# A fused fp32 transformer kernel on one core: router in plain fp32 with the tokens as stationary side, routing reordered, and the layer ends rearranged

## What is computed

```python
def grouped_moe(x, w_router, b_router, w_gate, w_up, w_down):        # first block, twice
    scores = softmax(x @ w_router + b_router)
    grp = scores.reshape(-1, 4, 4)
    g_sel = argmax(sum(top_k(grp, 2)[0], -1))                          # the best group
    top_w, top_i = top_k(grp[g_sel], 2); top_w = top_w / sum(top_w)
    for e in range(16):
        y = y + gate[:, e:e + 1] * ((silu(x @ w_gate[e]) * (x @ w_up[e])) @ w_down[e])

def hier_moe(h, w_rg, b_rg, w_re, b_re, w_gate, w_up, w_down):         # second block
    g_sel = argmax(softmax(h @ w_rg + b_rg)); e_val, e_idx = top_k((h @ w_re + b_re)[g_sel], 2)
# after it, in the second block:
    x = x + sigmoid(x @ w_ple_gate) * (p @ w_ple_proj)
```

## Time and profile before

| | us |
|---|---|
| median of 3 runs (lowest, highest) | 1481.27 (1480.82, 1482.70) |
| the profiled execution | 1480.01 |
| its span from the first to the last instruction | 1478.3 |
| PE, PEld, DVE, ACT, POOL busy | 1396.9, 1000.5, 607.5, 498.2, 53.8 |
| mean granted clock of TensorE | 0.982 |
| share of the chain that ended last: PE, DVE, ACT, issue | 88%, 5%, 4%, 2% |

### The profile page before, as it was taken

The page is one execution under the profiler, slowest core; times in us unless marked ns, Lnnn a source line. Parts: engine busy times, 40 slices in busy tenths (PEclk is TensorE's granted clock), DMA queues, the critical chain, the costliest instruction groups (busy, mean ns, idle before and its releaser), DMA issues.

```text
span 1478.3 us, 20927 instructions
## 1 busy us (share of the span) xinstructions
PE 1396.9 (94%) x8927; PEld 1000.5 (68%) x8927; DVE 607.5 (41%) x1001; ACT 498.2 (34%) x695; POOL 53.8 (4%) x95
## 2 busy tenths in 40 slices
PE   7999998999997999998999999799999989999977
PEld 5788976555554788986655554788787765555546
DVE  4677435111114585646111111657766561111124
ACT  5454434111113544443211111466565331111123
POOL 5000000000001000000000000000000000000000
PEclk9999999999999999999999999999999999999989
DMA  9556458999999455647899999453443769999970
GB/s 326 198 166 205 148 212 327 423 421 421 421 420 343 139 170 171 206 168 311 331 420 421 421 420 410 172 171 115 142 143 129 280 248 412 421 421 420 421 294 29
DMA packets 90807, 422.71 MB, mean 286 GB/s; under 512 B 7068, under 2 KB 7232, under 8 KB 53840
## 3 DMA queue, kind: packets, MB, share of 16 engines
q1 hardware_dynamic: 86528, 407.92, 70.8%
q0 software_dynamic: 4176, 13.30, 2.6%
HBM read 420.15 MB, written 1.05 MB: 285 GB/s over the span
## 4 chain that ended last, share of the span: by engine, by line
PE 88%; DVE 5%; ACT 4%; issue 2%; POOL 0%; DMA 0%; DVEq 0%; POOLq 0%; ACTq 0%
PE ps L1055 23%; PE ps L1091 12%; PE ps L753 5%; PE ps L754 5%; PE ps L758 5%; PE ps L972 4%; PE ps L1103 4%; PE ps L867 3%; PE ps L801 3%; PE ps L874 3%; PE ps L868 3%; PE ps L802 3%; PE ps L806 3%; PE ps L1080 1%; PE ps L914 1%
## 5 line engine op out<-in xcount | busy, mean ns | idle before, releaser
L1782 DVE TENSOR_TENSOR raw_low<-raw,w_high 128x1024 fp32r<-128x1024 f32 x198 | 237.4, 1223 | 171.2 <-ACT w_high L1440 170.5
L1440 ACT ACTIVATE w_high<-raw 128x1024 fp32r<-128x1024 f32 x198 | 206.6, 1058 | 258.6 <-PE ps L758 115.2
L2067 DVE TENSOR_TENSOR hid<-silu_g,ps 128x256 f32<-128x256 f32 x48 | 29.6, 616 | 259.8 <-PE ps L1055 259.8
L753 PE MATMUL ps<-w_high,act_high 128*128 128x512 f32 x272 | 110.6, 407 | 6.4 <-DVE raw_low L1782 3.6
L2075 DVE SCALAR_TENSOR_TENSOR out_low<-ps,stats,out_high 128x512 fp32r<-128x512 f32 x48 | 36.1, 751 | 182.3 <-ACT out_high L1546 182.3
L754 PE MATMUL ps<-raw_low,act_high 128*128 128x512 f32 x272 | 108.4, 399 | 0.0
L758 PE MATMUL ps<-w_high,act_low 128*128 128x512 f32 x272 | 103.3, 393 | 0.0
L1055 PE MATMUL ps<-raw,own_odd 128*64 128x256 f32 x800 | 91.6, 380 | 0.0
L1546 ACT ACTIVATE out_high<-ps,stats 128x512 fp32r<-128x512 f32 x48 | 33.0, 687 | 161.5 <-PE ps L1091 161.5
L867 PE MATMUL ps<-act_high,w_high 128*128 128x256 f32 x288 | 81.7, 287 | 5.4 <-issue 3.4
L1541 ACT ACTIVATE spread<-ps 128x288 fp32r<-128x288 f32 x48 | 19.7, 411 | 186.7 <-PE ps L1080 186.7
(11 more groups left out here) (411 smaller groups left out, 2570.8 us busy)
## 6 DMA issues: line engine op xcount, KB each, us to landing
raw<-in_w_up SPq DMA_DIRECT2D x46, 1024.0 KB, 11.3
raw<-in_w_in SPq DMA_DIRECT2D x44, 1024.0 KB, 9.2
raw<-in_w_gate SPq DMA_DIRECT2D x44, 1024.0 KB, 13.1
raw<-in_w_down SPq DMA_DIRECT2D x41, 1024.0 KB, 16.7
work<-in_w_down SPq DMA_DIRECT2D x23, 1024.0 KB, 19.7
work<-in_w_gate SPq DMA_DIRECT2D x21, 1024.0 KB, 7.9
w_lent<-in_w_gate SPq DMA_DIRECT2D x18, 1024.0 KB, 13.0
w_lent<-in_w_down SPq DMA_DIRECT2D x14, 1024.0 KB, 14.8
```

What stands on the lines that cost most here:

```text
L753: pe.matmul(bank[:, t, :], xh, wh, start=(k == 0), stop=False)
L1440: A(split_unit(n)[0], raw_unit(n), ACT.Copy).then_inc(high_ready, 1)
L1782: V.tensor_tensor(split_unit(n)[1], raw_unit(n), split_unit(n)[0].bitcast(F32), ALU.subtract).then_inc(low_ready, 1)
```

## The change

The diff, cut to its core:

```diff
-        plan_in(slots, L + turned_input + "0", L + turned_input + "1", L + "routerT", L + "router", L + "pos")
+        plan_in(slots, L + turned_input + "0", L + turned_input + "1", L + "router", L + "pos")
...
-    plan_job("2.x2T0", "2.x2T1")
-    plan_dense([a["w_ple_proj_2"][0].rearrange("(c p) n -> p c n", p=P)], "2.pp0", "2.pp1")
-    plan_dense([rows(a["w_ple_gate_2"][0], j) for j in range(4)], "2.pg0", "2.pg1")
+    plan_dense([a["w_ple_proj_2"][0].rearrange("(c p) n -> p c n", p=P)], "2.pp0", "2.pp1", slots=(H_SLOT, Y_SLOT))
+    plan_in(SUM_SLOTS, "2.x2T0", "2.x2T1")
+    plan_dense([rows(a["w_ple_gate_2"][0], j) for j in range(4)], "2.pg0", "2.pg1", slots=SUM_SLOTS)
...
-        NARROW = DEPTH * RANK + 2 * NE + SH + 4
+        NARROW = DEPTH * RANK + SH
+        router_w = sb("router_w", [P, KC, 2 * NE + 4])
...
+            def router(name, names, m, c0, width):
+
+                begin(name)
+                for t in range(TT):
+                    pe.wait_ge(S["front_turned"], TT * m + t + 1)
+                    pe.wait_ge(S["back_turned"], TT * m + t + 1)
+                    for c in range(KC):
+                        i = pe.matmul(slot_ps(name)[:, t * width:t * width + width], tokens_T[:, c, t * P:t * P + P], router_w[:, c, c0:c0 + width],
+                                      start=(c == 0), stop=(c == KC - 1))
+                        if c == 0:
+                            frees(i, names[t])
+                full(i, name)
...
                 for s in range(SLOTS):
                     pe.wait_ge(free[s], moe_at[m][1][s])
+                for _ in range(2):
+                    pe.matmul(ps[:, 1, 0:T], ident[:], tri[:, 0, :], start=True, stop=True)
...
-                    turn_tiles(x, (L + "xT0", L + "xT1"), S["normed"], TT * (3 * l - 1), idle=(8, 0))
-                dense_cols(L + "qk", head=(L + "xT0", L + "xT1"))
+                    turn_tiles(x[:, 0:1, :], (L + "xT0",), S["normed"], TT * (3 * l - 1))
+                second = (lambda: turn_tiles(x[:, 1:2, :], (L + "xT1",), S["normed"], TT * (3 * l - 1) + 1)) if l else None
+                dense_cols(L + "qk", head=(L + "xT0", L + "xT1"), between=second)
...
-            turn_tiles(h_tok, ("2.xT0", "2.xT1"), S["normed"], TT * 3 * DEPTH, idle=(14, 0))
+            turn_tiles(h_tok, ("2.xT0", "2.xT1"), S["normed"], TT * 3 * DEPTH)
...
-            turn_tiles(x, ("2.x2T0", "2.x2T1"), S["moe_added"])
             operand_ready("2.pT")
             dense_rows(("2.pp0", "2.pp1"), 1, (p_high, p_low))
+            turn_tiles(x, ("2.x2T0", "2.x2T1"), S["moe_added"])
...
                 for e in range(NE + 2):
                     if e >= 2:
                         output(e - 2)
+                    if e == NE:
+                        split(SPLIT - LATE)
...
-                    tiles_high(act_high, names[t:t + 1], t)
+                    wait_full(act, names[t])
+                    A(tokens_T[:, 0:KC // 2, t * P:t * P + P], slot_banks(names[t])[:, 0, :].rearrange("p (c s) -> p c s", s=P),
+                      ACT.Copy).then_inc(S["front_turned"], 1)
                     A(regrouped(x_tok[0][:, t, :]), runs(src[:, t, :]), ACT.Copy).then_inc(S["tok_high"], 1)
-                    A(y_acc[:, t, :], x[:, t, :], ACT.Copy, scale=scale).then_inc(S["residual_ready"], 1)
+                    if t == 0:
+                        residual_copied(0, scale)
...
-                narrow_copied(L + "router", NE, routT)
                 act.wait_ge(S["router_max"], l + 1)
                 A(probs, probs, ACT.Exp).then_inc(S["router_exp"], 1)
+                residual_copied(1, ALPHA)
...
                 V.tensor_tensor(probs, e_logits, r_max.to_broadcast([P, TT, NE]), ALU.subtract).then_inc(S["router_max"], 1)
+                ranks(groups(e_logits))
                 dve.wait_ge(S["router_exp"], l + 1)
-                ranks(groups(probs))
...
-                V.tensor_reduce(most, src[:, TT * NE:(TT + 1) * NE], AX, ALU.max)
-                frees(V.tensor_tensor(at_place, src[:, 0:TT * NE].rearrange("p (t n) -> p t n", t=TT), pick, ALU.mult), name)
+                link(V.tensor_tensor(at_place, src[:, 0:TT * NE].rearrange("p (t n) -> p t n", t=TT), pick, ALU.mult))
+                chosen(0, 0).then_inc(picks_made[m], 1)
+                frees(V.tensor_reduce(most, src[:, TT * NE:(TT + 1) * NE], AX, ALU.max), name)
+                chosen(0, 1)
                 wait_released(dve, name)
-                choose(0).then_inc(picks_made[m], 1)
...
                     if 0 < e <= NE:
                         hidden_copied(e - 1)
+                    if e == NE:
+                        split(HEAD)
...
                 route_one(l)
+                token_low(1, x, l)
                 place(l)
+                gates_one()
```

More of the change, by code:

```diff
@@ L741, in high_made, with dense_cols @@
                     pe.wait_ge(S["turned_high"], turn_no[name])
-            def dense_cols(name, src=MAIN, after_two=None, head=None):
+            def dense_cols(name, src=MAIN, after_two=None, head=None, between=None):
                 nonlocal n
@@ L762, in dense_cols @@
                     for t in range(TT):
+                        if t == 1 and between is not None:
+                            between()
                         high_made(head[t])
@@ L936, in narrow_turned @@
                     pe.matmul(dst, nl[:, c, :], act_high[:, c, 0:T], start=False, stop=False)
-                if head is not None:
-                    operand_ready(*head)
                 for c in range(KC):
@@ L1280, in _ @@
                 turn_tiles(x, (L + "x2T0", L + "x2T1"), S["normed"], TT * (3 * l + 1), idle=(2, 7))
-                narrow(L + "router", N_R, NE, (L + "x2T0", L + "x2T1"), routT)
+                router(L + "router", (L + "x2T0", L + "x2T1"), l, 0, NE)
                 sums_started(l)
@@ L1409, in _ @@
             turn_tiles(h_tok, ("2.x1T0", "2.x1T1"), S["normed"], TT * (3 * DEPTH + 2), idle=(2, 4))
-            narrow("2.router", N_RE, NE + 4, ("2.x1T0", "2.x1T1"), routT)
+            router("2.router", ("2.x1T0", "2.x1T1"), DEPTH, NE, NE + 4)
             sums_started(DEPTH)
@@ L1555, in experts_own @@
                         places_turned(e)
-                split(2)
                 if m == DEPTH:
@@ L1993, in choose, with chosen @@
             def choose(q):
-                for t, h in ((t, h) for t in range(TT) for h in range(2)):
+                for h in range(2):
+                    i = chosen(q, h)
+                return i
+            def chosen(q, h):
+                for t in range(TT):
                     i = V.tensor_tensor(picked[q % 2][:, t, :, h, :], slot_no[:].unsqueeze(1).to_broadcast([P, QUAD, OWN]),
@@ L2384, in _ @@
             route_two()
+            token_low(1, h_tok, DEPTH)
             place(DEPTH)
```

120 lines of the change are left out of this document (60 added, 60 removed).

## The result

| | before | after |
|---|---|---|
| median of 5 runs each, us (lowest, highest) | 1481.27 (1479.59, 1483.57) | 1493.53 (1486.78, 1495.41) |
| the profiled execution, and its span | 1480.01, 1478.3 | 1494.78, 1493.1 |
| mean granted clock of TensorE | 0.982 | 0.966 |
| PE busy | 1396.9 | 1407.5 |

What follows compares the result with a forecast made beforehand. PE was taken as the bound, with 88% of the chain and unchanged expert-loop products. Start -0.3, routings +0.6, ends -1.0, -1.0 and +2.1, late tile +0.45 gave +0.85 on 1481.27: 1482.1 us, range 1475.0 to 1488.5.

Steps and rivals of the forecast that it cites:

- The routings: Three routings: earlier logits, later residual and gather, clock gain in stages 0 and 1; 0.0, 0.0 and +0.6 us.
- Rival (a): Routings: PE's 2.2 us idle lowers the clock, residual at half clock, +1.7 us per routing, 1487.2 us; chance 0.27.
- A router product: Routing: one product with 128 tokens stationary and 16 columns moving takes 0.27 us, 2.16 per token tile.
- The two products: Ahead of the gather: two unused products cost 0.9 us; full clock in the gather returns 1.3 in stages 0 and 1.
- The end of stage 0: Layer end without eight unused products: dense work starts earlier but partly at half clock, -1.0 us.
- The end of stage 1: Layer end: first dense product 3.3 us earlier, half clock takes back 2.3, so -1.0 us, bounds -2.5 and +0.3.
- ACT's wait for the late tile: End of stage 1: ACT's `split(4)` waits for the second dense tile, delaying its last output and PE's sums, +0.45 us.
- The end of stage 2: Last layer end: `2.pp` goes first, the tile conversion loses its cover, +2.1 us, bounds +1.0 and +4.
- the uncovered conversion: End of stage 2: ACT 1.1 us and DVE 1.3 on tile 1, no longer under `2.pp`, idle PE 2.4 us.
- PE back earlier (b): Ends of stages 0 and 2: PE issues 2.9 us after its sums, -4.6 us, 1477.5 us; chance 0.15.
- The clock early at all ends (c): All three layer ends: full clock returns early, -3.4 us, 1478.7 us; chance 0.12.
- start: Start of the kernel: the narrow split covers 384 columns instead of 672, shortening PE's wait, -0.3 us.

Runs made afterwards that it cites:

- The run with the residual ahead: The changed kernel with the residual copy of tile 1 put back ahead of the exponential on ACT; 1485.47 us, ratio 1.002 to the kernel before.
- The kernel with the wide router: The changed kernel with tile 1's residual copy back ahead of ACT's exponential and router columns moved six times over; 1478.95 us, ratio 0.9977 to before.
- its twin with the old last end: The kernel with the wide router, residual copy also ahead, plus the old order at the end of stage 2 alone; 1475.93 us, ratio 0.9958 to before.

## Why the prediction was wrong

The sum in which it failed, step by step:

- **The routings, priced 0.0, 0.0 and +0.6, were +0.95, +2.78 and +3.45.** This is the failed step: 7.2 of the 14.8 us between the two profiles. The order of events was right: logits 1.1 us earlier against the tile (0.7 forecast: transposed at 227.83, read at 231.99, where it was 228.10 and 233.32), a PE gap of 1.94 us (2.2 forecast), a residual that ends last, a gather later by 2.3 to 3.3 us against the last transpose (12.88 to 15.22 in routing 0) where 1.3 was taken. What was wrong is the clock: "PE's residual products, 3.70 us" took 5.93, 6.29 and 5.96, which is 7.1 us more over the three. Rival (a) had this fall with +1.7 per routing and 0.27, and named the gap as its cause; the gap alone was followed by a fall in two routings of three, and the router's products without it in three of three. The argument "Against it: products fill PE right up to both ends of the gap" turned the wrong way: with the narrow products the clock fell even without the gap, and with the wide ones and no gap the residual ran at full clock. The forecast looked at whether PE is busy and not at what it moves.
- **A router product, taken as 0.27 us from the counting products, took 0.23** (1.86 for the eight of a tile at full clock). The Trainium skill, "TensorE: Matmul & The Clock Gate", section "LDWEIGHTS (loading the stationary operand)", gave an estimated 3.4 us for the 32 loads, the row-based term was 4.3; the rows have 1.86 + 2.04 = 3.9, and would have 3.7 had the second tile not run in part at half clock. That six times the columns cost 0.06 us agrees with that section, in which the load goes by the stationary columns alone.
- The same page of the Trainium skill, section "What's actually happening", says that the clock follows how busy PE has been. A reader takes from it that a PE without gaps keeps its clock. The run with the residual ahead shows otherwise: no gap over 0.38 us ahead of the residual, and 6.71 us for it.
- **The two products, +0.9 with -1.3 for the clock.** Both effects exist. In after the gather took 4.10, 5.12 and 4.10 us, before 5.49, 5.48 and 3.99: -1.4, -0.4 and +0.1. That is less than the 1.3 taken twice, and taking them out gained 1.4 us over three routings.
- **The end of stage 0, -1.0, was +1.35 in the profile and 0.0 over 13 profiles.** PE's return was later (6.56 us behind the sums where 5.63 was taken) and the half clock lasted beyond 480, not to 477.6. Removing eight products without a use gained nothing here: what follows ran at half clock in their place.
- **The end of stage 1, -1.0, was right.** The first dense product came 2.9 us sooner after the last sum (3.3 forecast), and the half clock behind it took 1.6 us back (2.3 allowed): -1.3, and -2.1 over 13 profiles. The +4.73 in the profile comes from the untouched stretch behind it: +6.0, of which the same code shows 3.0 between two executions. It was no part of the forecast. Whether the change has a share in it is open (2.8 us over 13 profiles).
- **ACT's wait for the late tile, +0.45, was +0.25:** the wait was seen in its place. Over the nine profiles that have it, it cost 0 to 1.2 us, 0.34 in the mean.
- **The end of stage 2, +2.1, was +1.52 in the profile,** but not by the forecast's parts. PE did not stop a second time behind the sums, as it had in before: its first product came 3.6 us after the last issue of the sums and it went on. So `2.pg` began 16.56 us after that issue, against 16.48 in before, and what was lost is the half clock at which it then started, behind its gap of 2.83 us. That is the bound "+4 (the clock falls again in the 2.4 us of idle)". The kernel with the wide router and its twin with the old last end, where PE does not stop twice either, differ by 2.05. That is the price of the uncovered conversion, near it partly by luck, since the twin's PE came back 0.7 us later. Over the profiles the end is 3.8 longer.
- **PE back earlier (b)** occurred at the last end only, as just said. PE's first issue behind the branch came 5.9 to 7.0 us after the last issue of the sums at the end of stage 0 in all 13 profiles, whatever stood there; at the last end 3.2 to 6.4. No run tests whether fetching the branch's target is the cause; the section of the Trainium skill that the prediction cites has that fetch only for a target outside what is already fetched. **The clock early at all ends (c)** did not occur.

Put together from means of profiles: routings +7.8 (62.2 over the two kernels with the changed routing, 54.4 over the three with the old), ends 0.0 + 0.7 + 3.8, late tile +0.3, start -0.9 (227.65 over ten, 228.57 over three): +11.7, where the medians differ by 12.3. That sum rests on few executions of each kernel, so its closeness is partly luck.

**What stays open:** why the same gap of 1.94 us brought a fall in two routings and not in the third, why stretches at half clock in the untouched code come and go between executions, and whether the new order at the end of stage 1 makes them more frequent. The runs show that it happens and what it costs, not by what rule.

## What to carry to other kernels

An edit that keeps PE busy with products of few columns can lower its clock for the large products behind them; read the granted clock of the stretch behind an edit, and where the width of the moving side hardly changes the time (here 1.86 us with 16 columns and 1.92 with 96), widen it. A step moved behind another on its engine is priced with the clock of what waits for it, not with its duration alone. Where one profile differs from another in code that nothing touched, take several executions before giving that difference a cause.

## What the runs showed of the hardware

- Sixteen records with 128 stationary columns in plain fp32 take 1.86 us with 16 moving columns and 1.92 with 96.
- With 16 or 20 moving columns the granted clock fell to the lower level within these products or up to 0.45 us behind them, in nine routings of nine, and from the first of them to the fall PE had no gap over 0.45 us (in stage 2 there is one of 1.72 ahead of the transposes, as with the wide router too); with 96 or 120 the residual behind them took 3.60 to 3.63 us in all 18 routings of the six kernels that also had the residual ahead, and with 16 or 20 columns and no wait 6.71, 5.38 and 5.13.
- The stretch of 1394 PE instructions in stage 2 spent between 13.7 and 31.2 us at the lower level. Identical code took 258.2 and 261.2 us.
- Behind the expert branch PE issued nothing for 5.5 to 6.6 us at the end of stage 0 and for 2.8 to 6.0 at the end of stage 2, with no wait that the profile names in 13 profiles of 13 and in ten of 13.
- One product of 256 columns added at a layer end moved the median by 2.7 us, and four moved it by -0.5.
